# Streaming the moving rows of the float32r products, and the bank that they fill, from the last column to the first

## The reference

```python
def swiglu(x, w_in, w_out):
    g, u = jnp.split(x @ w_in, 2, axis=-1)
    return (jax.nn.silu(g) * u) @ w_out
...
    for i in range(DEPTH):
        h = h + 0.5 * swiglu(rms_norm(h, ffn1_norm[i]), ffn1_w_in[i], ffn1_w_out[i])
        ...  # mixer of this layer
        h = h + 0.5 * swiglu(rms_norm(h, ffn2_norm[i]), ffn2_w_in[i], ffn2_w_out[i])
    return rms_norm(h, final_norm)
...
    x = x + swiglu_2(rmsnorm(x, norm_ffn[l]), w_gate_up[l], w_down[l])
```

## Time and profile before

| | |
|---|---|
| Time, median of two runs | 2819.22 us (2818.82 to 2819.62) |
| Span of the profiled execution, first to last instruction | 2817.5 us |
| Time of an execution less that span | 1.7 us (from the median) |
| TensorE busy | 2790.9 us, 99% of the span |
| VectorE, GpSimd, ScalarE busy | 1657.6, 1571.1, 1346.4 us |
| DMA | 267.91 MB, 95 GB/s on average |
| Granted TensorE clock, mean | 0.999 of 2.4 GHz |

### The profile page before, as it was taken

How to read it: one execution, slowest core, us unless ns; L and a number is a source line. 1 busy time by engine, 2 the same in 40 slices (tenths; PEclk the granted TensorE clock), 3 DMA queues, 4 the chain that set the end, 5 groups by cost and what they waited for, 6 DMA issues and landing times.

```text
span 2817.5 us, 45558 instructions
## 1 busy us (share of the span) xinstructions
PE 2790.9 (99%) x16386; PEld 2391.3 (85%) x16386; DVE 1657.6 (59%) x2703; ACT 1346.4 (48%) x2076; POOL 1571.1 (56%) x872
## 2 busy tenths in 40 slices
PE   8999999999999999999999999999999999999999
PEld 6998877899889998888999886665688888799987
DVE  6777147677616774135777416579788464477730
ACT  5554257555425554243555334557444444455531
POOL 6775445677547774444777443158633373367743
PEclk9999999999999999999999999999999999999999
DMA  3234322232332233332223332112222342123332
GB/s 136 105 104 115 103 82 82 91 104 104 111 99 90 104 109 105 100 106 89 91 104 120 101 94 77 53 53 66 71 89 70 103 149 75 53 103 107 109 98 77
DMA packets 80685, 267.91 MB, mean 95 GB/s; under 512 B 11168, under 2 KB 13216, under 8 KB 80560
## 3 DMA queue, kind: packets, MB, share of 16 engines
q1 hardware_dynamic: 77904, 262.01, 28.4%
q10 hardware_dynamic: 2656, 4.26, 0.5%
HBM read 263.09 MB, written 2.10 MB: 94 GB/s over the span
## 4 chain that ended last, share of the span: by engine, by line
PE 94%; DVE 3%; ACT 1%; issue 1%; DMA 0%; POOL 0%; ACTq 0%; SPq 0%; DVEq 0%
PE bank L460 17%; PE bank L462 17%; PE bank L461 17%; PE bank L716 10%; PE bank L718 10%; PE bank L717 10%; PE bank L547 1%; PE bank L548 1%; PE bank L549 1%; PE bank L1635 1%; PE bank L2047 1%; PE bank L2915 1%; PE bank L2647 0%; PE bank L2056 0%; PE bank L2627 0%
## 5 line engine op out<-in xcount | busy, mean ns | idle before, releaser
L448 POOL TENSOR_TENSOR w_lo<-w_stage,w_hi 128x1024 fp32r<-128x1024 f32 (+1 forms) x228 | 535.2, 2353 | 714.0 <-ACT w_hi L424 713.5
L424 ACT ACTIVATE w_hi<-w_stage 128x1024 fp32r<-128x1024 f32 (+1 forms) x412 | 421.0, 1027 | 367.2 <-PE bank L462 303.5
L803 POOL TENSOR_TENSOR w_lo<-w_stage,w_hi 128x1024 fp32r<-128x1024 f32 (+1 forms) x176 | 327.3, 1859 | 202.1 <-ACT w_hi L424 202.1
L460 PE MATMUL bank<-xg_hi,w_hi 128*128 128x512 f32 x976 | 396.2, 406 | 5.0 <-DVE h_raw L1063 3.8
L461 PE MATMUL bank<-xg_lo,w_hi 128*128 128x512 f32 x976 | 381.2, 391 | 0.0
L462 PE MATMUL bank<-xg_hi,w_lo 128*128 128x512 f32 x976 | 381.2, 391 | 0.0
L455 POOL TENSOR_TENSOR w_lo<-w_stage,w_hi 128x1024 fp32r<-128x1024 f32 (+1 forms) x96 | 234.9, 2453 | 261.7 <-ACT w_hi L424 217.3
L460 PE MATMUL bank<-h_hi,w_hi 128*128 128x512 f32 x880 | 342.3, 389 | 0.0
L461 PE MATMUL bank<-h_lo,w_hi 128*128 128x512 f32 x880 | 342.3, 389 | 0.0
L462 PE MATMUL bank<-h_hi,w_lo 128*128 128x512 f32 x880 | 342.3, 389 | 0.0
L718 PE MATMUL bank<-xg_hi,w_lo 128*128 128x256 f32 x1056 | 299.2, 283 | 0.0
(11 more groups left out here) (530 smaller groups left out, 6599.0 us busy)
## 6 DMA issues: line engine op xcount, KB each, us to landing
w_stage<-w_up SPq DMA_DIRECT2D x220, 512.0 KB, 4.2
w_stage<-w_down SPq DMA_DIRECT2D x80, 512.0 KB, 3.5
w_stage<-merge SPq DMA_DIRECT2D x36, 512.0 KB, 3.4
w_stage<-w_down SPq DMA_DIRECT2D x40, 384.0 KB, 3.2
w_stage<-hg_qfg SPq DMA_DIRECT2D x12, 512.0 KB, 3.4
w_stage<-rec_r SPq DMA_DIRECT2D x8, 512.0 KB, 3.5
w_stage<-rec_y SPq DMA_DIRECT2D x8, 512.0 KB, 3.4
w_stage<-rec_out SPq DMA_DIRECT2D x8, 512.0 KB, 3.4
```

Source lines behind the costliest of these rows:

```text
L424: act.activation(w_hi[:, r, 0:w], w_stage[:, r, 0:w], ACT.Copy).then_inc(w_hi_ready, 1)
L448: pool.tensor_tensor(w_lo[:, r, 0:w], w_stage[:, r, 0:w], f32(w_hi[:, r, 0:w]), ALU.subtract).then_inc(w_lo_ready, 1)
L460: pe.matmul(out, w_hi[:, r, c], hi, start=start, stop=False)
L803: pool.tensor_tensor(w_lo[:, r, cs], w_stage[:, r, cs], f32(w_hi[:, r, cs]), ALU.subtract).then_inc(w_lo_ready, 1)
```

## The change

Two lines are added. `three_passes` and `product` turn their output and their moving operands round: each access pattern starts at the last element of the row and steps back by one. Moving columns and output columns are turned together, so every token's result lands where it did. The stationary operands (`w_hi`, `w_lo`, `s_w` blocks) keep their direction. Every other matmul is as it was.

```diff
     def three_passes(pe, out, r, j, hi, lo, start, stop):
 
         c = slice(j * P, (j + 1) * P)
+        out, hi, lo = out[:, ::-1], hi[:, ::-1], lo[:, ::-1]
         pe.matmul(out, w_hi[:, r, c], hi, start=start, stop=False)
         pe.matmul(out, w_hi[:, r, c], lo, start=False, stop=False)
         return pe.matmul(out, w_lo[:, r, c], hi, start=False, stop=stop)
...
         def product(out, w, v):
             (wh, wl), (xh, xl) = w, v
+            out, xh, xl = out[:, ::-1], xh[:, :, ::-1], xl[:, :, ::-1]
             for k in range(4):
                 c = slice(k * P, (k + 1) * P)
                 pe.matmul(out, wh[:, c], xh[:, k, :], start=k == 0, stop=False)
```

## The result

The changed kernel takes 2861.2 us (median of two runs, 2859.8 to 2862.6) against 2819.2: ratio 1.0143, 95% interval 1.0119 to 1.0167. TensorE's mean granted clock is 0.999 of 2.4 GHz in both profiled executions, so the clock is not what differs.

What follows compares the result with a forecast made beforehand. The prediction took TensorE, streaming one column per clock, to bound the kernel. It summed 2817.5 us of span, 0 for the change and 1.7 us beside the span to 2819.2 us, range 2783 to 2855 us.

Steps and rivals of the forecast that it cites:

- What bounds the kernel: Whole kernel: TensorE, busy 2790.9 of 2817.5 us and 94% of the chain, so any matmul price change counts in full.
- The count and the lever: Matmuls through three_passes and product: 14256 of 16386, 2412 us; 1 ns on each is 14.3 us or 0.5%.
- within 2%: Whole kernel: measured time would differ from before by no more than about 2%, 56 us; chance 0.79.
- The price of a backward matmul: Every touched matmul: zero extra, bounded by 2.5 ns each, 36 us upward or downward; chance 0.78.
- fixed part of 11 to 13 ns: Each matmul in down projections and block products: time independent of its columns, which stream at one per clock.
- The write: Bank writes of touched matmuls: turned alike, 512 or 256 columns still between additions to a column; no added price.
- the rival of half pace: Every touched matmul: columns pass at half the pace if read or write pairs need step +1; 2127 us more, 4946 us; chance 0.16.
- The dearer start: Head of each touched matmul: a set-up of another 13.3 ns, 190 us in all, 3009 us; chance 0.04.

Runs made afterwards that it cites:

- m2_places: Bench outside the kernel, no other engine at work: offsets of moving row and weight block, and weight width, varied; at 512 columns aligned, 227.8 ns forward, 234.2 backward.
- e6_aligned: Kernel before, all forward, with only the sums of tokens (xsum) moved from 64 bytes past a 1024-byte boundary onto it: 2828.3 us, ratio 1.0031.
- e2_write: Kernel before with only the outputs of three_passes and product turned round, moving rows read forward: 2820.0 us, ratio 0.9998.
- m3_blocks: Bench outside the kernel: widths varied, and 512-column rows cut into groups of g elements, reversing group order or the inside: 227.8 to 267.5 ns a matmul.
- e5_place: Kernel before, all forward, with only xsum moved from 64 to 192 bytes past a 1024-byte boundary: 2802.2 us, ratio 0.9935.
- e7_best: e5_place with only the 3168 products on the tokens themselves read and written backward: 2811.2 us, ratio to the kernel before 0.9967.

## Why the prediction was wrong

- What bounds the kernel: right. The whole difference lies in the six lines, with no new wait.
- The count and the lever (14256 matmuls, 14.3 us for each ns): right; the average price was 2.9 ns. That the time stayed within 2%, which had 0.79, was luck: the prediction had it so because nothing changes, and it came out so because 6.6 ns are 3% of a matmul and the two kinds of block product moved opposite ways.
- The price of a backward matmul: the failed step. The prediction took zero with the words that "with equal counts the nearest row is the unchanged one", and bounded it by 2.5 ns, the gap between the two kinds of block product. The counts (columns, neighbours, distance between writes) are equal, but the order in which a row goes through its 256-byte periods is a further quantity, and the runs showed it to matter: up to +6.6 ns at 512 columns, +2.1 on sums, -1.6 on the tokens at 256. With it fell the sentence that the time goes into columns and "not into weight loads or memory", with a fixed part of 11 to 13 ns: in m2_places the places of row and weights alone moved the part beyond the columns from 7.8 to 14.1 ns at 256 columns forward, and from 14.2 to 24.0 at 512. The gap of 2.5 ns in the earlier trace rows was itself the sign of it: the two kinds differ in place (64 bytes past the boundary, and on it), and e6_aligned, which removes that difference, brings both to 120.0. I read the row as the noise of a quantity when it was one sample of an effect, at one width, and carried it to 512 columns. 2861.2 us lies 6 us above the range.
- The write: right. e2_write is at 0.9998, and the rival of half pace is out on both sides: with adjacent weight columns no series of 512 was above 240.8 ns, except the one with groups of 16 reversed inside, 267.5, and the first series of each bench, whose first matmuls start 427 ns apart before they fall to 227. The Trainium skill's rule on the 8-byte lines (Advanced Engine Details and Errata, section PSUM Cachelines) holds in its reading by lines: a reversed row of the bank keeps both elements of each line together and costs nothing (226.7 ns in e2_write). For the moving read the Trainium skill's Advanced Engine Details and Errata, section SBUF Cachelines, gives 16-byte lines and full performance while consecutive accesses hit the same line. That agrees with the free reversal inside 4 elements (228.0 ns), but does not tell the rest: all of the orders of m3_blocks with g of 4 and more hit each line four times in a row, and they lie between 227.8 and 267.5 ns.
- The dearer start: the direction was right and the mechanism half so. There is a part beyond the columns that grows, from 13.3 to 20.0 ns at 512 columns, by 6.7 and not by 13.3; and it is not a fixed set-up, since it shrinks at 256 columns on the boundary. Its chance of 0.04 was too low, and so was that of anything slower by more than 36 us and less than 2%.
- What stays open: what in the memory makes the backward order dear. That the forward price is a matter of moving row and next weights together is shown (the weights' offset alone moves it from 227.8 to 234.1 ns). That the backward price has the same cause was only argued. For it: at 256 columns it moves with the weights' offset by up to 2.2 ns, and at 512 it stops growing where the stream has lasted as long as the load. Against it: at 512 columns it did not react to the weights' offset in 11 of 12 pairs, nor by more than 0.9 ns to their width. The two benches that were to isolate it did not. What carries the level over from one matmul to the next was not looked into.

## What to carry to other kernels

Where TensorE is dense with float32r products, the start-to-start distance beyond columns / 2.4 GHz is worth a look of its own: here 7 to 20 ns a matmul, 0.5% of the kernel for each ns on all of them, moved by the address of the moving buffer modulo 256 bytes, the order in which it is read, and the neighbouring products. A bench with one series for each place finds the candidates in a single run, but the winner has to be timed in the kernel, since neighbouring products change each other's price: e5_place kept its promise of 17 us and e7_best fell 14 short of its own. And a small difference between two near-identical groups in a trace should be explained before it is used as a bound for anything else.

## What the hardware showed unexpectedly

- A 512-column float32r matmul read backward costs 233.3 ns against 226.7 forward; written backward, 226.7.
- At 512 columns the price forward repeats at a shift of 64 elements (227.3, 227.2, 227.3 ns at 0, 64 and 128) and is low (227.7 to 228.0) when moving row and weight block have the same offset in it, at five of six offsets tried. At 256 columns the row at 48 elements with the weights on the boundary was the cheapest, 114.4 ns against 120.7 with both on it.
- Reversing 16 elements inside groups is the worst order tried, 267.5 ns; reversing 4 is free.
- Weight columns taken with a step of 63 or 65 elements make a 256-column matmul cost 234 to 236 ns against 119 to 121.
- A series of identical matmuls can settle at 114.4 or at 118.7 ns; in the kernel the same 35 sums took 113.1 ns each beside forward products and 117.7 beside backward ones.
- Two matmuls on 64 rows each, in different halves of the partitions and into different banks, ran at the same time: 230 ns a pair.
